# Products over 256 tokens: one 512-column pass for the two halves of the activation

## The chip, the cores and the metric

The program runs on one core of a Trainium2 chip. The metric is the device time of one execution in microseconds (us), over three executions of the same build; less is better.

## The reference

Everything is float32. A sequence of 256 tokens (16 meta tokens go ahead of them, so the first half works on T = 272 rows) of width 2048 passes through four mixers and two feed-forward layers:

- block 1, layer 0: `h = h + mla(rms(h))` (low-rank queries and keys, 16 heads, chunked mask), then `h = h + (silu(g) * u) @ w_down`, with `g, u = split(rms(h) @ w_gu)` and 5632 hidden features;
- block 1, layer 1: `h = h + ((scan(gates(conv(xb))) * gelu(yb)) @ w_o)`, with `xb, yb = split(rms(h) @ w_in)`, then a second feed-forward; from here on only the 256 real tokens are needed;
- a final norm, then block 2, even layer: 8 heads of grouped attention and 8 heads of differential attention (`softmax(s1) - lam * softmax(s2)`) times `silu(gate)`, then `@ w_out_even`;
- block 2, odd layer: 16 heads of windowed attention times `silu(gate)`, `@ w_out_odd`, and a last norm.

Nearly all arithmetic is in products of a weight matrix with the activations of all tokens. The accuracy asked for is near that of float32.

## The kernel before

**The products.** Activations lie with features on the 128 partitions and tokens along the row. Each operand is held as two float32r tensors, a rounded high part and the remainder (low part): `XHt`, `XLt` for the normed input of a stage, `HHt`, `HLt` for the input of its output projection, and `WHt`, `WLt` for the weights. A weight tile of 128x128 times 128 input features of all tokens is three matmuls into one PSUM bank, lines 988 to 990: high weight by high activation, high weight by low activation, low weight by high activation. Each loads its own stationary operand. The moving operand has 272 columns in the first half of the program (`REG`) and 256 later (`REGM`). For the values of the attention heads the operands are swapped (lines 983 to 985, `VT`).

**Units and groups.** Weights come from HBM in 501 units of 1 MB or less, each four 128-row slices by four 128-column tiles as a rule: 16 tile products, 48 matmuls. Each unit is loaded into `raw` by a DMA, split by ACT into `WHt` (line 1194, `split_high`) and by DVE into `WLt` (line 1478, `split_low`). All three have three places. TensorE can start unit n only when DVE has made its `WLt`; ACT can split unit n+3 only when TensorE has finished unit n. A group (`Plan.group`) is four units, or as many as the sum over the input features needs, into four PSUM banks, one per output tile. The eight banks go round in a queue: a group or an attention step takes the bank that was given back longest ago, and TensorE waits (`own`) until that bank's last content has been read.

**The way out.** When a group has ended, its four banks are read by DVE in the feed-forward, the recurrent layer and the gates: `scaled_out` (line 1552) multiplies by the row of inverse norms. `gu_out` does it for the feed-forward, followed by silu on ACT (1304), a product on DVE (1692), the high part on ACT (1308) and the low part on DVE (1694). `qk_out`, `gate_out` and `yg_out` do it for the other products. In output projections `residual` (line 1638) adds the bank to `h`; where a norm follows, ACT makes the next `XHt` (1221) and squares (1237), DVE the next `XLt` (1481), and GpSimd adds the squares (2059). All of that stands ahead of the group's closing `split_high` in ACT's order.

**The order of the work.** `make_plan` writes one list of steps; each engine walks the list and issues its own part of every step, strictly in order. `p.after(k, fn)` puts attention steps k+1 units further on. In the odd layer a head is `s_step` (scores, lines 1122 and 1123, then bias, maximum, exponential and norm), `t_step` (four transposes, line 1130, copied to SBUF by ACT at line 1375) and `v_step` (weighing of values, lines 1139 and 1140). For a pair of heads there are two groups: queries and keys first, then values and gates (`pair_products`).

## Time and profile before

| | |
|---|---|
| median of three executions | 3121.19 us (3121.07 to 3123.58) |
| the profiled execution, its own time | 3122.28 us |
| its span (first to last instruction) | 3120.5 us |
| TensorE matmuls, weight loads | busy 99% and 98% of the span, 25096 records each |
| DVE, ACT, GpSimd | busy 56%, 45%, 4% |
| DMA | 534.89 MB, mean 171 GB/s |
| granted TensorE clock | 0.998 of 2.4 GHz |

The record of a matmul reaches from its first column to its last result, and those of neighbours overlap, so its busy share alone doesn't say how fast TensorE works: the distance from one start to the next does. The chain of waits names what each instruction on it waited for last. "Idle before" is time in which an engine had nothing running, and what ended it.

### The profile page before, as it was taken

Reading aid. Unit: us, or ns where it says so; the run is one execution under the profiler, and the core shown is the slowest. Engines: PE = TensorE matmul, PEld = TensorE weight load, DVE = VectorE, ACT = ScalarE, POOL = GpSimd, SP = SyncE. Lnnn points to the kernel's source line nnn. Section 1 sums busy time; section 2 is a strip of 40 time slices with the busy share of each in tenths; the row PEclk is TensorE's granted clock in tenths of the full one; section 3 lists DMA queues with packets and bytes.
Section 4 is the critical chain, followed back from the end, with each engine's and each line's share of the span. In section 5 each row is a group of like instructions: output and inputs, shape, how many; then the busy total and the mean of one; then the engine's idle time right before and its main releaser. Section 6 shows DMA issues by size and latency. Waiting matters only on the chain.

```text
span 3120.5 us, 56102 instructions
## 1 busy us (share of the span) xinstructions
PE 3088.2 (99%) x25096; PEld 3044.3 (98%) x25096; DVE 1749.4 (56%) x2053; ACT 1394.7 (45%) x1469; POOL 120.1 (4%) x127
## 2 busy tenths in 40 slices
PE   9999999999999999999999999999999999999998
PEld 8889999999999999999999999999999999999998
DVE  6665544444445567755554554555666665555554
ACT  5444433333333456754333333345455554444443
POOL 1001000000000011110000000002000000000000
PEclk9999999999999999999999999999999999999999
DMA  6224454455454554445555555554444445444443
GB/s 227 101 104 149 177 176 175 176 176 176 176 176 174 178 184 185 169 176 191 188 189 189 184 185 186 189 183 178 155 149 149 175 163 189 163 176 163 164 175 122
DMA packets 77888, 534.89 MB, mean 171 GB/s; under 512 B 8528, under 2 KB 11088, under 8 KB 14928
## 3 DMA queue, kind: packets, MB, share of 16 engines
q1 hardware_dynamic: 76640, 528.94, 47.7%
q8 instruction: 197, 3.23, 0.4%
q10 hardware_dynamic: 1008, 2.37, 0.2%
q14 instruction: 43, 0.35, 0.0%
HBM read 529.18 MB, written 2.10 MB: 170 GB/s over the span
## 4 chain that ended last, share of the span: by engine, by line
PE 95%; issue 3%; DVE 1%; ACT 1%; POOL 0%; DMA 0%; SPq 0%; DVEq 0%; ACTq 0%; POOLq 0%
PE PB L988 28%; PE PB L989 28%; PE PB L990 28%; PE PB L983 2%; PE PB L985 2%; PE PB L984 2%; PE PB L1050 0%; PE PB L1090 0%; PE PB L1139 0%; PE PB L1140 0%; PE PB L1051 0%; PE PB L1122 0%; PE PB L1123 0%; DMA raw<-in_mla_in 0%; PE PB L1130 0%
## 5 line engine op out<-in xcount | busy, mean ns | idle before, releaser
L1478 DVE TENSOR_TENSOR WLt<-raw,WHt 128x2048 fp32r<-128x2048 f32 (+2 forms) x506 | 1142.6, 2262 | 938.1 <-ACT WHt L1194 937.7
L1194 ACT ACTIVATE WHt<-raw 128x2048 fp32r<-128x2048 f32 (+2 forms) x506 | 955.4, 1890 | 1298.8 <-PE PB L990 1244.1
L988 PE MATMUL PB<-XHt,WHt 128*128 128x256 f32 (+1 forms) x5072 | 1450.1, 286 | 8.4 <-ACT S L1375 5.8
L989 PE MATMUL PB<-XLt,WHt 128*128 128x256 f32 (+1 forms) x5072 | 1437.5, 283 | 0.0
L990 PE MATMUL PB<-XHt,WLt 128*128 128x256 f32 (+1 forms) x5072 | 1436.0, 283 | 0.0
L988 PEld LDWEIGHTS PB<-XHt,WHt 128*128 128x128 f32 x5072 | 956.0, 188 | 15.3 <-ACT S L1375 8.0
L989 PEld LDWEIGHTS PB<-XLt,WHt 128*128 128x128 f32 x5072 | 955.5, 188 | 2.7 <-issue 1.4
L990 PEld LDWEIGHTS PB<-XHt,WLt 128*128 128x128 f32 x5072 | 954.8, 188 | 0.0
L988 PE MATMUL PB<-HHt,WHt 128*128 128x256 f32 (+1 forms) x2432 | 690.6, 284 | 1.7 <-DVE WLt L1478 0.6
L989 PE MATMUL PB<-HLt,WHt 128*128 128x256 f32 (+1 forms) x2432 | 689.2, 283 | 0.0
L990 PE MATMUL PB<-HHt,WLt 128*128 128x256 f32 (+1 forms) x2432 | 688.5, 283 | 0.0
L988 PEld LDWEIGHTS PB<-HHt,WHt 128*128 128x128 f32 x2432 | 458.0, 188 | 3.0 <-DVE WLt L1478 0.8
L989 PEld LDWEIGHTS PB<-HLt,WHt 128*128 128x128 f32 x2432 | 457.8, 188 | 0.4 <-issue 0.2
L990 PEld LDWEIGHTS PB<-HHt,WLt 128*128 128x128 f32 x2432 | 457.6, 188 | 0.0
L2059 POOL TENSOR_TENSOR acct<-acct,sqt 128x256 f32<-128x256 f32 (+1 forms) x107 | 86.4, 815 | 2785.4 <-ACT sqt L1237 2777.4
L983 PE MATMUL PB<-WHt,XHt 128*128 128x256 f32 (+1 forms) x512 | 147.9, 289 | 0.6 <-DVE S L1570 0.6
L985 PE MATMUL PB<-WLt,XHt 128*128 128x256 f32 (+1 forms) x512 | 143.8, 281 | 0.0
L984 PE MATMUL PB<-WHt,XLt 128*128 128x256 f32 (+1 forms) x512 | 143.5, 280 | 0.0
L1552 DVE TENSOR_TENSOR S<-PB,Rt 128x256 f32<-128x256 f32 (+1 forms) x313 | 114.5, 425 | 26.7 <-PE PB L990 26.5
L983 PEld LDWEIGHTS PB<-WHt,XHt 128*128 128x128 f32 (+1 forms) x512 | 93.9, 183 | 5.1 <-issue 3.4
L1304 ACT ACTIVATE S<-S 128x544 f32<-128x544 f32 (+1 forms) x44 | 28.4, 646 | 157.6 <-DVE S L1552 157.6
L984 PEld LDWEIGHTS PB<-WHt,XLt 128*128 128x128 f32 (+1 forms) x512 | 93.5, 183 | 1.9 <-issue 0.7
(207 smaller groups left out, 1496.7 us busy)
## 6 DMA issues: line engine op xcount, KB each, us to landing
raw<-in_gu SPq DMA_DIRECT2D x176, 1024.0 KB, 4.8
raw<-in_dn SPq DMA_DIRECT2D x88, 1024.0 KB, 4.8
raw<-in_odd_in SPq DMA_DIRECT2D x64, 1024.0 KB, 4.8
raw<-in_even_in SPq DMA_DIRECT2D x52, 1024.0 KB, 4.9
raw<-in_lru_in SPq DMA_DIRECT2D x28, 1024.0 KB, 4.8
raw<-in_mla_o SPq DMA_DIRECT2D x16, 1024.0 KB, 4.9
raw<-in_lru_o SPq DMA_DIRECT2D x16, 1024.0 KB, 4.9
raw<-in_even_o SPq DMA_DIRECT2D x16, 1024.0 KB, 4.8
```

The lines of the kernel that those rows point to most:

```text
L983: t.matmul(o, ah, wh, start=first, stop=False)
L984: t.matmul(o, al, wh, start=False, stop=False)
L985: m = t.matmul(o, ah, wl, start=False, stop=last)
L988: t.matmul(o, wh, ah, start=first, stop=False)
L989: t.matmul(o, wh, al, start=False, stop=False)
L990: m = t.matmul(o, wl, ah, start=False, stop=last)
L1194: a.activation(hi, r, ACT.Copy).then_inc(s_hi, 1)
L1304: a.activation(gg, gg, ACT.Silu).then_inc(sems["silu"], 1)
L1478: v.tensor_tensor(lo, r, hi.bitcast(f32), sub).then_inc(s_lo, 1)
L1552: v.tensor_tensor(dst, PB[b][:, 0:n], by, mult).then_inc(s_bank[b], 1)
L2059: g.tensor_tensor(acc[which][:, t0:T], acc[which][:, t0:T], sq[slot][:, t0:T], add).then_inc(sems["acc"], 1)
```

## The change

A tile kind replaces the flag for swapped operands: "rows" (as before), "values" (swapped) and "wide". For a wide tile the high and the low part of 256 activations are one moving operand of 512 columns, since `Xt` and `Ht` now hold both parts of a feature slice side by side. It meets the high weight in one matmul that fills the whole bank, two halves of 256. The low weight meets the high part in a second matmul, added to the bank's first half. So a tile product is two matmuls instead of three, with the same number of columns. The bank's two halves are added on the way out: ACT copies the second half to SBUF (`halves`), DVE adds the first half to it, and then multiplies two tiles at once by the row of inverse norms (`wide_out`). In output projections DVE adds both halves to `h`, one after the other.

Wide are: all gate and up products of the second feed-forward; three of the four column groups of the four later output projections and of each part of the second feed-forward's; the `y` tiles of the recurrent layer but the last pair; all gates of the attention layers; queries and keys of the odd layer. What works on 272 tokens stays, and so do the fourth column group of each projection, the first attention's queries and the differential attention's queries and keys. In the first attention of the even layer the weighing steps come one unit later, in the odd layer scores and transposes one unit earlier.

```diff
+WIDE = [(128 * c, 128, M0, NT, "wide") for c in range(4)]
...
+    def halves(g, tiles, *where):
+        for i in tiles:
+            p.mark("half", "half", g, i)
+        for i in tiles[1::2]:
+            p.mark("wide", "wide", g, i)
+        p.step("halves", g, tiles, *where)
+
     def out_proj(kunits, t0, fresh, stage, finish=(), scaled=False):
         for m in range(4):
-            g = p.group(kunits, REGM if t0 else REG, "H", 0, fresh if m == 0 else None)
+            g = p.group(kunits, REG if not t0 else WIDE if m < 3 else REGM, "H", 0, fresh if m == 0 else None)
...
-                g = p.group(4, REGM if t0 else REG, "X", 0, stage if j == 0 else None)
+                g = p.group(4, WIDE if t0 else REG, "X", 0, stage if j == 0 else None)
                 for i in range(4):
                     p.give("g", g, i)
+                if t0:
+                    buffers = (2 * (turn % 2), 2 * (turn % 2) + 1)
+                    halves(g, (0, 1, 2, 3), buffers, [last[turn % 2]] if turn > 1 else [])
...
-        tiles = (REG[0:2] if q < 8 else []) + ([REGM[0 if q == 8 else 2], REGM[1 if q == 8 else 3]] if q else [])
+        tiles = (REG[0:2] if q < 8 else []) + (WIDE[2:4] if 0 < q < 8 else REGM[0:2] if q else [])
...
-        g = p.group(4, REGM, "X")
+        g = p.group(4, REGM[0:2] + WIDE[2:4], "X")
...
-        p.after(3, lambda v=v, q=q: (v(0), t_step(("e", 2 * q + 1))))
-        p.after(4, lambda v=v: v(1))
+        p.after(4, lambda v=v, q=q: (v(0), t_step(("e", 2 * q + 1))))
+        p.after(5, lambda v=v: v(1))
...
     def pair_products(name, sides, fresh=None):
-        g = p.group(4, REGM, "X", 0, fresh)
+        odd = name[0] == "C"
+        g = p.group(4, WIDE if odd else REGM, "X", 0, fresh)
         p.close()
...
+        if odd:
+            halves(g, (0, 1, 2, 3), ("q", "k"), done("q_done"))
...
-        g = p.group(4, VT + REGM[:2], "X")
+        g = p.group(4, VT + WIDE[0:2], "X")
...
-        pair_products(("C", q), {2: lambda s=s: s(0), 3: lambda s=s, q=q: (t_step(("o", 2 * q)), s(1)),
+        pair_products(("C", q), {1: lambda s=s: s(0), 2: lambda s=s, q=q: (t_step(("o", 2 * q)), s(1)),
                                  4: lambda v=v, q=q: (v(0), t_step(("o", 2 * q + 1))), 5: lambda v=v: v(1)},
...
-        XHt, XLt = sb("XHt", KD * T, f32r), sb("XLt", KD * T, f32r)
-        HHt, HLt = sb("HHt", KD * T, f32r), sb("HLt", KD * T, f32r)
+        Xt, Ht = sb("Xt", 2 * KD * T, f32r), sb("Ht", 2 * KD * T, f32r)
...
-                        if swap:
+                        if kind == "wide":
+                            o = two(bank[:, :])
+                            both = (X2 if src == "X" else H2)[:, k0 + kk, :, t0:T]
+                            t.matmul(o, wh, both, start=first, stop=False)
+                            m = t.matmul(o[:, 0, :], wl, ah, start=False, stop=last)
+                        elif kind == "values":
...
+            def halves(g, tiles, dst, free):
+                for k in free:
+                    a.wait_ge(*when(*k))
+                for at, i in enumerate(tiles):
+                    b = plan.bank["g", g, i][0]
+                    a.wait_ge(*when("tile", g, i))
+                    a.activation(wide_pairs(dst)[at // 2][:, at % 2, :], PB[b][:, NT:2 * NT], ACT.Copy).then_inc(sems["half"], 1)
...
+            def wide_out(g, tiles, dst, r=None):
+                pairs = wide_pairs(dst)
+                for at, i in enumerate(tiles):
+                    b, x = plan.bank["g", g, i][0], pairs[at // 2][:, at % 2, :]
+                    v.wait_ge(*when("half", g, i))
+                    v.tensor_tensor(x, PB[b][:, 0:NT], x, add).then_inc(s_bank[b], 1)
+                if r:
+                    v.wait_ge(*when(*r))
+                for x, i in zip(pairs, tiles[1::2]):
+                    v.wait_ge(*when("out", "g", g, i - 1))
+                    v.wait_ge(*when("out", "g", g, i))
+                    v.tensor_tensor(x, x, RO.unsqueeze(1).to_broadcast([128, 2, NT]), mult).then_inc(sems["wide"], 1)
...
+                if plan.groups[g][2][i][4] == "wide":
+                    then(v.tensor_tensor(h[:, mt, t0:T], PB[b][:, NT:2 * NT], h[:, mt, t0:T], add))
+                    v.wait_ge(s_vec, vec[0])
                 v.tensor_tensor(h[:, mt, t0:T], PB[b][:, 0:T - t0], h[:, mt, t0:T], add).then_inc(s_bank[b], 1)
```

TensorE at the end of a pair of the odd layer (`Xt` is the new tensor of both parts). Before, transposes of the first head and scores of the second stand between the values-and-gates group and the next pair's first group:

```order
L988 MATMUL PB<-XHt,WHt 128x256
L989 MATMUL PB<-XLt,WHt 128x256
L990 MATMUL PB<-XHt,WLt 128x256
L1130 MATMUL PB<-cst,S 128x128 x4
L1122 MATMUL PB<-S 128x256
L1123 MATMUL PB<-S 128x256
```

Now the same steps stand inside the values-and-gates group, with its last unit (swapped products, then wide ones) behind them:

```order
L1004 MATMUL PB<-Xt,WHt 128x512
L1005 MATMUL PB<-Xt,WLt 128x256
L1155 MATMUL PB<-cst,S 128x128 x4
L1147 MATMUL PB<-S 128x256
L1148 MATMUL PB<-S 128x256
L1008 MATMUL PB<-WHt,Xt 128x256
L1009 MATMUL PB<-WHt,Xt 128x256
L1010 MATMUL PB<-WLt,Xt 128x256
```

The gate product of three matmuls has become two, one of 512 columns, and one unit of products now lies between these steps and the next group. Over the whole program TensorE's list goes from 24521 to 20761 rows.

ACT at the end of the second feed-forward, before (silu, high part, the four weight splits of the next four units):

```order
L1304 ACTIVATE S<-S 128x512
L1308 ACTIVATE HHt<-S 128x2x256
L1194 ACTIVATE WHt<-raw 128x2048 x4
L1304 ACTIVATE S<-S 128x512
L1308 ACTIVATE HHt<-S 128x2x256
```

and now:

```order
L1281 ACTIVATE S<-PB 128x256 x4
L1337 ACTIVATE S<-S 128x512
L1341 ACTIVATE Ht<-S 128x2x256
L1219 ACTIVATE WHt<-raw 128x2048 x4
L1281 ACTIVATE S<-PB 128x256 x4
```

Four copies of half a bank (L1281) stand ahead of each silu, and so ahead of the split of the weights that comes after the high part.

## Rows read from the trace of the kernel before

**Rows 1.** The page: busy time, then the chain that ended last

```profile
PE 3088.2 (99%) x25096; PEld 3044.3 (98%) x25096; DVE 1749.4 (56%) x2053; ACT 1394.7 (45%) x1469; POOL 120.1 (4%) x127
...
PE 95%; issue 3%; DVE 1%; ACT 1%; POOL 0%; DMA 0%; SPq 0%; DVEq 0%; ACTq 0%; POOLq 0%
```

**Rows 2.** Windows: second feed-forward (256 columns), first (272); start:end, length, busy (count)

```profile
core 0: us, PE busy (x) PEld busy (x) DVE busy (x) ACT busy (x) POOL busy (x), PEclk, DMA share, GB/s
1430.00:1590.00 160.00, 160.00 (x1362) 160.00 (x1361) 86.53 (x72) 63.78 (x44) 0.00 (x0) 1.00 0.54 189
...
350.00:500.00 150.00, 150.00 (x1198) 150.00 (x1198) 77.13 (x66) 55.36 (x40) 0.00 (x0) 1.00 0.49 174
```

**Rows 3.** Chain in order of time: plain float32 products, start and length

```profile
1305.46 1.83 PE PB L1090 x8
...
2205.72 0.86 PE PB L1103 x2
```

**Rows 4.** Groups of instructions, shapes apart: count, busy us, mean ns

```profile
L989 PE MATMUL PB<-XLt,WHt 128*128 128x256 f32 x3104 | 869.2, 280 | 0.0
...
L989 PE MATMUL PB<-XLt,WHt 128*128 128x272 f32 x1968 | 568.3, 289 | 0.0
```

**Rows 5.** Timeline of TensorE: stationary operand of 16 columns, then of 128

```profile
151.51 0.28 PE L983 MATMUL PB<-WHt,XHt 128*16 128x256 f32 x1
151.63 0.28 PE L984 MATMUL PB<-WHt,XLt 128*16 128x256 f32 x1
151.74 0.28 PE L985 MATMUL PB<-WLt,XHt 128*16 128x256 f32 x1
151.86 0.28 PE L983 MATMUL PB<-WHt,XHt 128*128 128x256 f32 x1
```

**Rows 6.** TensorE's waits for ACT: total us, times, longest

```profile
PE PB L988 <- ACT S L1375: 6.3, 12, 0.5
```

**Rows 7.** Timeline: start of a pair of the odd layer

```profile
2661.62 0.28 PE L990 MATMUL PB<-XHt,WLt 128*128 128x256 f32 x1
2661.82 0.58 ACT L1375 ACTIVATE S<-PB 128x512 f32<-128x512 f32 x1
...
2662.44 0.39 PE L988 MATMUL PB<-XHt,WHt 128*128 128x256 f32 x1 [0.54 <-ACT S L1375]
```

**Rows 8.** Groups of instructions, shapes apart: reading and scaling of banks

```profile
L1552 DVE TENSOR_TENSOR S<-PB,Rt 128x256 f32<-128x256 f32 x184 | 66.5, 419 | 10.0 <-PE PB L990 9.9
...
L1638 DVE TENSOR_TENSOR ht<-PB,ht 128x256 f32<-128x256 f32 x96 | 36.0, 425 | 16.8 <-PE PB L990 16.8
...
L1692 DVE TENSOR_TENSOR S<-S 128x512 f32<-128x512 f32 x22 | 15.2, 693 | 2.3
...
L1356 ACT ACTIVATE S<-PB,sml 128x256 f32<-128x256 f32 x26 | 10.7, 460 | 0.0
```

**Rows 9.** Timeline of DVE and ACT: end of a group, second feed-forward

```profile
1463.95 1.43 DVE L1552 TENSOR_TENSOR S<-PB,Rt 128x256 f32<-128x256 f32 x4 [0.34 <-PE PB L990]
...
1468.68 2.29 DVE L1478 TENSOR_TENSOR WLt<-raw,WHt 128x2048 fp32r<-128x2048 f32 x1 [1.11 <-ACT WHt L1194]
...
1466.75 1.90 ACT L1194 ACTIVATE WHt<-raw 128x2048 fp32r<-128x2048 f32 x1
```

**Rows 10.** Timeline of DVE and ACT: end of a column group, second feed-forward's last projection

```profile
2130.18 1.50 DVE L1638 TENSOR_TENSOR ht<-PB,ht 128x256 f32<-128x256 f32 x4 [0.27 <-PE PB L990]
...
2139.65 4.49 DVE L1478 TENSOR_TENSOR WLt<-raw,WHt 128x2048 fp32r<-128x2048 f32 x2 [5.89 <-ACT WHt L1194]
...
2130.64 1.71 ACT L1221 ACTIVATE XHt<-ht,sml 128x256 fp32r<-128x256 f32 x4 [3.06 <-DVE ht L1638]
...
2137.72 3.71 ACT L1194 ACTIVATE WHt<-raw 128x2048 fp32r<-128x2048 f32 x2
```

**Rows 11.** Timeline of DVE: the first column group there, then the even layer's projection

```profile
2113.24 1.50 DVE L1638 TENSOR_TENSOR ht<-PB,ht 128x256 f32<-128x256 f32 x4 [0.27 <-PE PB L990]
...
2121.81 4.49 DVE L1478 TENSOR_TENSOR WLt<-raw,WHt 128x2048 fp32r<-128x2048 f32 x2 [5.49 <-ACT WHt L1194]
...
2566.80 1.50 DVE L1638 TENSOR_TENSOR ht<-PB,ht 128x256 f32<-128x256 f32 x4
...
2573.33 4.50 DVE L1478 TENSOR_TENSOR WLt<-raw,WHt 128x2048 fp32r<-128x2048 f32 x2 [2.95 <-ACT WHt L1194]
```

More of the change, by code:

```diff
@@ L632, in make_plan @@
         p.mark("silu", "silu", "A", q)
-        p.step("gate_silu", gb, ("A", q), ("out", "g", g, 3))
+        p.step("gate_silu", gb, ("A", q), ("wide", g, 3))
         q_in = ("out", "g", g, 1)
@@ L729, in pair_products @@
         p.mark("silu", "silu", name)
-        p.step("gate_silu", "gp", (name,), ("out", "g", g, 3))
+        p.step("gate_silu", "gp", (name,), ("wide", g, 3))
         cur["silu"] = ("silu", name)
@@ L814, in flat @@
             return x.rearrange("p a n -> p (a n)")
-        h, XH, XL, HH, HL = three(ht), three(XHt), three(XLt), three(HHt), three(HLt)
+        h = three(ht)
+        X2, H2 = (t[:, :].rearrange("p (k s n) -> p k s n", k=KD, s=2) for t in (Xt, Ht))
+        XH, XL, HH, HL = X2[:, :, 0, :], X2[:, :, 1, :], H2[:, :, 0, :], H2[:, :, 1, :]
         ident, ones, perm = cst[:, 0:128], cst[:, 128:256], cst[:, 256:384]
@@ L869, in build_program, with wide_pairs @@
         RO = R[:, M0:T]
+        def wide_pairs(dst):
+            return [yg] if dst == "yg" else [two(buf[x] if x in buf else gbuf[x][:, 0:2 * NT]) for x in dst]
         def last_sq(mt):
@@ L966, in unit @@
                 for k, ti in order:
-                    for c0, wd, t0, tn, swap in (tiles[ti],):
+                    for c0, wd, t0, tn, kind in (tiles[ti],):
                         kk = ku * nk + k
@@ L1302, in gu_out @@
                 gg, u = two(gbuf[2 * turn][:, 0:2 * n]), two(gbuf[2 * turn + 1][:, 0:2 * n])
-                a.wait_ge(*when("out", "g", g, 1))
+                a.wait_ge(*when(*(("wide", g, 1) if t0 else ("out", "g", g, 1))))
                 a.activation(gg, gg, ACT.Silu).then_inc(sems["silu"], 1)
@@ L1423, in _ @@
                     c_split(*x)
+                elif what == "halves":
+                    halves(*x)
                 elif what == "uq_out":
@@ L1687, in gu_out @@
                     v.wait_ge(*when(*r))
-                for i in range(4):
-                    scaled_out((gg, u)[i // 2][:, i % 2, :], g, i, None, n, R[:, t0:T])
+                if t0:
+                    wide_out(g, (0, 1, 2, 3), (2 * turn, 2 * turn + 1))
+                else:
+                    for i in range(4):
+                        scaled_out((gg, u)[i // 2][:, i % 2, :], g, i, None)
                 v.wait_ge(*when("silu", l, j))
-                v.wait_ge(*when("out", "g", g, 3))
+                v.wait_ge(*when(*(("wide", g, 3) if t0 else ("out", "g", g, 3))))
                 v.tensor_tensor(u, u, gg, mult).then_inc(sems["gu"], 1)
@@ L1828, in kA_scale, with gate_out, qk_out @@
                 v.tensor_tensor(buf["kA"], buf["kA"], PB[b][:, :], mult).then_inc(s_bank[b], 1)
-            def gate_out(b, g, free):
+            def gate_out(b, g):
+                wide_out(g, (2, 3), (b,))
+            def qk_out(g, free, r):
                 for k in free:
                     v.wait_ge(*when(*k))
-                for i in range(2):
-                    scaled_out(two(buf[b])[:, i, :], g, 2 + i, None, NT, RO)
-            def qk_out(g, free):
-                for k in free:
-                    v.wait_ge(*when(*k))
-                for i in range(4):
-                    r = ("out", "sp", "ln_odd") if i == 0 else None
-                    scaled_out(two(buf[("q", "k")[i // 2]])[:, i % 2, :], g, i, r if odd[0] else None, NT, RO)
-            odd = [False]
+                if plan.groups[g][2][0][4] == "wide":
+                    wide_out(g, (0, 1, 2, 3), ("q", "k"), r)
+                else:
+                    for i in range(4):
+                        scaled_out(two(buf[("q", "k")[i // 2]])[:, i % 2, :], g, i, None, NT, RO)
             def rows(q, before):
```

32 lines of the change are left out of this document (18 added, 14 removed).

## The prediction

> **What bounds the kernel.** I read the page first. TensorE is busy for 99% of the span, and 95% of the chain of waits is its matmuls; DVE is at 56% and ACT at 45% [rows 1]. The time is therefore a number of matmuls times their pace, plus the few places where TensorE stands. The pace I took from windows without attention. In the second feed-forward 1362 matmuls overlap 160 us; two of them were already running, so the distance from start to start is 160/1360 = 117.6 ns for 256 columns. In the first it is 150/1196 = 125.4 ns for 272 [rows 2]. At the granted 2.4 GHz, one column per cycle, 256 columns take 106.7 ns and 272 take 113.3. So 10.9 and 12.1 ns of each matmul are not columns. The change keeps every column and removes matmuls, so it can gain only from this remainder, and all depends on what the remainder is.
>
> **Part 1, fewer and longer matmuls.** The wide tile products are 22 groups x 64 in the second feed-forward, 92 feature slices x 12 tiles in the projections, 224 in the recurrent layer, 256 in the even layer's gates, 768 in the odd layer: 1408 + 1104 + 224 + 256 + 768 = 3760, which is what TensorE's list loses (24521 to 20761). Each was 3 x 117.6 = 352.9 ns.
>
> No row shows a 512-column matmul of this type. The two paces bound it. If the remainder belongs to the matmul, the long one takes 213.3 + 10.9 = 224.2 ns and a product saves 10.9. If the pace grows per column as it does from 256 to 272 columns, by 7.8/16 = 0.49 ns, it takes 117.6 + 256 x 0.49 = 242.4 ns, against 235.3 for two: a loss of 7.1 ns. The ends are +41 us and -27 us over 3760.
>
> The nearest rows of 512 columns are plain float32 products, at two cycles per column: eight records of 272 columns in 1.83 us are 228.8 each, 2.1 over their cycles; two of 512 in 0.86 us are 430 each, 3.3 over their 426.7 [rows 3]. There, what is over hardly grows with length: it is per matmul. It isn't the weight load either, since with a stationary operand of 16 columns the distance is still (151.86 - 151.51)/3 = 0.117 us [rows 5]. I take the side of a cost per matmul, but not all of it: going by 272 against 256 columns, 1.2 ns more for 16 more, some grows. I count 9.2 ns saved per product, an estimate between these rows: 3760 x 9.2 = **34.6 us**.
>
> **Part 2, the moved steps.** TensorE waits 12 times for ACT's copy of transposed weights (L1375) [rows 6]: once per pair of the odd layer, 8, and 4 in the first attention. The transposes stood directly ahead of a group, and the group's third tile is given the bank that they had just filled. At one such place the start of the tile comes at 2662.44, 0.82 us after its predecessor at 2661.62 instead of 0.12 [rows 7], so 0.70 us is lost. Now a unit of products (5.6 us) follows the transposes, and the copy is long done when the bank comes round: 12 x 0.70 = **8.4 us** gained.
>
> The scores of the odd layer come one unit earlier, two units (11 us) behind the query group. Queries and keys are ready later than before: split of weights on ACT to 1.9 us, four copies of 0.46, the last add at 4.2, two multiplications of 0.69 to 5.6 us [rows 8]. 5 us remain. The softmax chain, scores to transposes, keeps its one unit. I count nothing.
>
> **Part 3, the longer way out.** ACT gets 166 copies of half a bank (88 in the feed-forward, 14 recurrent, 16 even, 48 odd), at the 0.46 us of a similar read, 76 us. DVE gets 83 multiplications of 512 elements at 0.69 (the 166 old multiplications become adds), 57 us, and 72 second adds in projections at 0.425, 31 us [rows 8]. The cover is TensorE: ACT goes to 48%, DVE to 60% of the time. What counts is how late `WLt` of the unit three ahead becomes. In the feed-forward the group ends near 1464.75, and the units in hand last 2 x 5.65 = 11.3 us, until 1476.05. The split of the high part starts at 1466.75 and DVE's low part ends at 1470.97 [rows 9]: 5.1 us of margin. Copies from -1.0 to +0.85 us, last add at 1.3, first product 2.0, silu 2.6, product 3.4, high part 4.05, split 5.95, low part 8.25, that is 2 us later than now: margin about 2.8 with the shorter units. Free; if this cover went, each of 22 groups would cost what is missing.
>
> One place is tight: the last projection of the second feed-forward, where ACT squares everything twice ahead of its split. The group ends near 2131.05, the units in hand last until 2142.35; the first of DVE's two low parts ends at 2139.65 + 2.29 = 2141.94 [rows 10]. Margin 0.4 us, and ACT is the one that is late (its split starts at 2137.72). Now each `XHt` waits for two adds; eight adds of 0.375 take until 2133.1, the fourth `XHt` ends at 2133.6 instead of 2132.35, 1.2 us later, and the two units are 0.3 us shorter. Missing: 1.1 us, at two of three column groups. At the first the adds begin at 2113.24, the units in hand last until 2125.4 and the low part ends at 2121.81 + 2.25 = 2124.1, a margin of 1.3, and 0.2 is missing. **2.5 us** lost. The other projections square once: their low part ends 8.8 us after the adds begin (2566.80 to 2575.6), a margin of 3.4, and nothing is missing [rows 11].
>
> **Sum.** Against the profiled execution's own 3122.28 us (span 3120.5): 3122.3 - 34.6 - 8.4 + 2.5 = 3081.8. That run lies 1.1 us above the median 3121.19, so **3081 us**.
>
> **Rivals.**
>
> *A. The remainder goes with the columns.* For it: a matmul's own record is 280 ns at 256 columns and 289 at 272 [rows 4]; less the paces, 162 and 164: the extra time lies within the record, not between records, as if the columns came more slowly than one per cycle. Then only the part that plain float32 products show, 2.1 to 3.3 ns, is saved: 3760 x 2.3 = 8.6 us, 3121.2 - 8.6 - 8.4 + 2.5 = **3107 us**. Against it: record ends are modelled, and at 272 columns the remainder should be 11.6, not 12.1. The Trainium skill (TensorE: Matmul & The Clock Gate, Back-to-back issue gap) gives columns/2.4 + 2.5 ns per matmul, which speaks against this change: it would save 2.5 x 3760 = 9.4 us, to 3106. The trace disagrees with its pace, 117.6 ns instead of 109.2. Chance 0.23.
>
> *B. The long matmul costs more than two short ones* (the other side). The growth of 0.49 ns per column holds on to 512: 242.4 ns. For it: it is the only slope that rows give for this type, and the moving operand is now two pieces that lie apart. Then 3121.2 + 26.7 - 8.4 + 2.5 = **3142 us**. It decides for slower by over 0.2% above 238.5 ns for the long matmul. Against: 0.49 is more than a cycle per column, which leaves a negative cost per matmul. Chance 0.15.
>
> *C. The merge gives nothing*: the chip treats the two-piece operand as two passes, and the change doesn't do what it says. The gain is the moved steps, 3121.2 - 5.9 = **3115 us**; a few short waits for DVE or ACT at group ends, of 0.1 us each at some 60 groups, would make that 3121. Chance 0.10.
>
> *D. More gain.* The remainder comes from a weight load that just fails to fit under 256 columns, and fits under 512: the long matmul takes 213.3 + 3.3, 18.7 ns saved, 70 us, **3045 us**. Rows 5 speak against it. Chance 0.06.
>
> **How the numbers follow.** My forecast (a cost per matmul) has 0.46. About 0.2%, 6 us, is what a measurement of this kernel can tell from no change: faster are my case, A and D, 0.75; within it is C, 0.10; slower B, 0.15. My own case runs from 3070 (12.1 ns saved) to 3091 (6.5 ns). The range takes in A and C and the nearer edge of B: 3060 to 3130, leaving out D and most of B.
>
> **What would show it.** In the window of the second feed-forward a tile product (two matmuls) every 341 to 344 ns is my case, 350 is A, 353 C, 360 B, 334 D. The record of the 512-column matmul should be about 387 ns (224 + 163), against 396 under A. The 12 waits for L1375 should be gone. In the last projection of the second feed-forward TensorE should wait about 1 us for `WLt` at two or three places, and nowhere in the other groups. The prediction is wrong if the product's pace lies above 350 ns, or if waits of TensorE for `WLt`, banks or queries add up to more than 5 us.

## The result, and the profile after

| | before | after |
|---|---|---|
| median of six executions each | 3122.07 us (3121.07 to 3123.58) | 3110.59 us (3108.75 to 3111.82) |
| ratio, 95% interval | | 0.9962 (0.9951 to 0.9973) |
| the profiled execution, span | 3122.28, 3120.5 us | 3111.64, 3109.8 us |

The changed kernel is faster by 11.5 us, inside the range, but the forecast was 41 us. The page of the changed kernel, busy time and the chain of waits (for before, rows 1):

```profile
PE 3080.9 (99%) x21336; PEld 2871.8 (92%) x21336; DVE 1828.5 (59%) x2208; ACT 1448.7 (47%) x1635; POOL 110.7 (4%) x127
...
PE 95%; issue 2%; DVE 1%; ACT 1%; POOL 1%; ACTq 0%; DVEq 0%; POOLq 0%
```

TensorE has 3760 records less and is still busy for 99% of the time: its busy time fell by only 7.3 us. DVE and ACT took on nearly what Part 3 said (59% and 47%). So the question is the pace. The same two windows as in [rows 2]:

```profile
core 0: us, PE busy (x) PEld busy (x) DVE busy (x) ACT busy (x) POOL busy (x), PEclk, DMA share, GB/s
350.00:500.00 150.00, 150.00 (x1197) 150.00 (x1196) 76.21 (x65) 56.09 (x39) 0.00 (x0) 1.00 0.49 174
1430.00:1590.00 160.00, 160.00 (x914) 139.45 (x913) 95.54 (x86) 73.55 (x73) 0.00 (x0) 1.00 0.52 189
```

In the second feed-forward 914 matmuls overlap 160 us, two of them were already running: 912/2 = 456 products, 350.9 ns each. Before it was 3 x 117.6 = 352.9. By the starts in the trace a unit of 16 wide products takes 5.613 us, 350.8 ns per product, against 5.6465 us, 352.9 ns. **A merged product saves 2.1 ns**, where 9.2 were counted. One row behind the other, the changed kernel's timeline of TensorE:

```profile
1499.95 0.39 PE L1004 MATMUL PB<-Xt,WHt 128*128 128x512 f32 x1
1500.18 0.28 PE L1005 MATMUL PB<-Xt,WLt 128*128 128x256 f32 x1
1500.30 0.40 PE L1004 MATMUL PB<-Xt,WHt 128*128 128x512 f32 x1
1500.54 0.28 PE L1005 MATMUL PB<-Xt,WLt 128*128 128x256 f32 x1
```

From a wide pass to the next matmul are 0.23 to 0.24 us, 232.5 ns on average from 1432 to 1660 us, from a narrow one 0.12 (118.3 ns). The narrow pass is nearly what it was; the wide pass costs 232.5, nearly the 235.2 of the two passes that it replaces. The waits of TensorE in the changed kernel (total us, times, longest), where [rows 6] stood:

```profile
PE PB L1004 <- DVE WLt L1513: 2.3, 3, 1.3
...
PE PB L1115 <- DVE S L1773: 1.7, 1, 1.7
...
PE PB L1013 <- DVE WLt L1513: 1.2, 1, 1.2
```

No wait for a copy of transposes is left; before there were 12, 6.3 us. New are waits for `WLt` (0.6 us before, 3.5 now) and 1.1 us more for `S` at the head of the recurrent layer's last gates (L1115; L1090 with 0.6 us before). Three of the four `WLt` waits stand behind the three merged column groups of the second feed-forward's last projection, the places of [rows 10, 11]:

```profile
2124.16 0.50 PE L1004 MATMUL PB<-Ht,WHt 128*128 128x512 f32 x1 [0.30 <-DVE WLt L1513]
...
2142.56 0.51 PE L1004 MATMUL PB<-Ht,WHt 128*128 128x512 f32 x1 [1.32 <-DVE WLt L1513]
...
2161.00 0.39 PE L1013 MATMUL PB<-Ht,WHt 128*128 128x256 f32 x1 [1.24 <-DVE WLt L1513]
```

The fourth, 0.67 us at the start of the recurrent layer's projection, was there before with 0.64.

The starts of the stages in the two traces say where the span's 10.7 us came from: up to the recurrent layer +1.9, recurrent layer with its projection +0.2, second feed-forward -0.3, even layer's products and attention -3.4, its projection -0.4, odd layer's products and attention -7.3, the rest -1.4. The two stages in which steps were moved hold -3.4 and -7.3, as much as the whole. In the second feed-forward, where half of all merges are, two things cancel: up to its last projection it is 3.7 us shorter (1792 merged products x 2.1 ns are 3.8), and the last projection, with its three waits, is 3.4 us longer. And the first 1124 us, where nothing is merged, became longer.

### The profile page after: what moved, and what is told of

The parts are those of the page before. It is cut to its first block, busy times and chain, and to the rows that moved or that the text cites. A ratio compares the mean times of both kernels' runs of the same rounds, so it can differ in the third digit from the quotient of the medians.

```text
span 3109.8 us, 49013 instructions
## 1 busy us (share of the span) xinstructions
PE 3080.9 (99%) x21336; PEld 2871.8 (92%) x21336; DVE 1828.5 (59%) x2208; ACT 1448.7 (47%) x1635; POOL 110.7 (4%) x127
## 4 chain that ended last, share of the span: by engine, by line
PE 95%; issue 2%; DVE 1%; ACT 1%; POOL 1%; ACTq 0%; DVEq 0%; POOLq 0%
PE PB L1004 27%; PE PB L1013 15%; PE PB L1015 15%; PE PB L1014 14%; PE PB L1005 13%; PE PB L1008 2%; PE PB L1010 2%; PE PB L1009 2%; PE PB L1147 0%; PE PB L1075 0%; PE PB L1164 0%; PE PB L1155 0%; PE PB L1165 0%; PE PB L1148 0%; POOL acct L2112 0%
## 5 line engine op out<-in xcount | busy, mean ns | idle before, releaser
L1004 PE MATMUL PB<-Xt,WHt 128*128 128x512 f32 x2656 | 949.9, 395 | 0.0
L1005 PE MATMUL PB<-Xt,WLt 128*128 128x256 f32 x2656 | 744.3, 280 | 0.0
L1013 PE MATMUL PB<-Xt,WHt 128*128 128x272 f32 (+1 forms) x2416 | 704.5, 292 | 2.5 <-DVE Xt L1516 1.9
L1015 PE MATMUL PB<-Xt,WLt 128*128 128x272 f32 (+1 forms) x2416 | 694.6, 287 | 0.0
L1014 PE MATMUL PB<-Xt,WHt 128*128 128x272 f32 (+1 forms) x2416 | 693.2, 287 | 0.0
L1004 PEld LDWEIGHTS PB<-Xt,WHt 128*128 128x128 f32 x2656 | 498.6, 188 | 101.2
L1005 PEld LDWEIGHTS PB<-Xt,WLt 128*128 128x128 f32 x2656 | 499.1, 188 | 0.2
L1013 PEld LDWEIGHTS PB<-Xt,WHt 128*128 128x128 f32 x2416 | 455.8, 189 | 13.2 <-DVE WLt L1513 3.0
L1014 PEld LDWEIGHTS PB<-Xt,WHt 128*128 128x128 f32 x2416 | 457.1, 189 | 2.3 <-issue 1.4
L1015 PEld LDWEIGHTS PB<-Xt,WLt 128*128 128x128 f32 x2416 | 456.7, 189 | 0.0
L1004 PE MATMUL PB<-Ht,WHt 128*128 128x512 f32 x1104 | 389.7, 396 | 2.6 <-DVE WLt L1513 2.3
L1013 PE MATMUL PB<-Ht,WHt 128*128 128x272 f32 (+1 forms) x1328 | 380.4, 286 | 1.2 <-DVE WLt L1513 1.2
L1014 PE MATMUL PB<-Ht,WHt 128*128 128x272 f32 (+1 forms) x1328 | 379.3, 286 | 0.0
L1004 PEld LDWEIGHTS PB<-Ht,WHt 128*128 128x128 f32 x1104 | 207.2, 188 | 53.8 <-DVE WLt L1513 3.7
L1013 PEld LDWEIGHTS PB<-Ht,WHt 128*128 128x128 f32 x1328 | 249.7, 188 | 1.8 <-DVE WLt L1513 1.4
L1014 PEld LDWEIGHTS PB<-Ht,WHt 128*128 128x128 f32 x1328 | 250.2, 188 | 0.0
L1015 PEld LDWEIGHTS PB<-Ht,WLt 128*128 128x128 f32 x1328 | 250.0, 188 | 0.0
L1005 PEld LDWEIGHTS PB<-Ht,WLt 128*128 128x128 f32 x1104 | 207.2, 188 | 0.3 <-issue 0.2
```

What stands on the lines that cost most here:

```text
L1004: t.matmul(o, wh, both, start=first, stop=False)
L1005: m = t.matmul(o[:, 0, :], wl, ah, start=False, stop=last)
L1013: t.matmul(o, wh, ah, start=first, stop=False)
L1014: t.matmul(o, wh, al, start=False, stop=False)
L1015: m = t.matmul(o, wl, ah, start=False, stop=last)
```

## The experiments

Medians are of repeated executions beside the kernel before on the same chip; the three programs of matmuls alone ran once each. Where runs of different sets are compared, their kernels before differ by up to 0.5 us (3122.07 to 3122.55).

### The pace of one matmul

A program of matmuls alone, 192 of each form, without waits:

```diff
+ for i in range(192): t.matmul(o[:, 0:256], W[:, w:w + 128], X4[:, k, i % 2, 16:272])
+ for i in range(192): t.matmul(o[:, 0:272], W[:, w:w + 128], X4[:, k, i % 2, 0:272])
+ for i in range(192): t.matmul(o[:, 0:n], W[:, w:w + 128], X[:, 512 * k:512 * k + n])
+ for i in range(192): t.matmul(o (two halves), W[:, w:w + 128], X4[:, k, :, 16:272])
```

> A kernel of matmuls alone, float32r, 160 to 192 in a row of each form, a new weight tile for each unless said; it computes nothing of the reference. Forms: 256, 272, 320, 384 and 512 columns; 512 as two pieces of 256; 256 with always the same weights; 256 with a stationary operand of 32 columns; 256 with every matmul opening its own sum; bfloat16 at 256 and 512 columns; 256 and 512 again beside a busy ScalarE and VectorE. Theory 1 (the part beyond one column per cycle goes with the columns at four bytes each, about 2 ns are per matmul): 512 columns 231 to 234 ns from start to start, 320 about 146, 384 about 175, bfloat16 109 at 256 and 216 at 512, and neither pieces, weights, the short stationary operand nor busy neighbours change 256 columns by over 2 ns. Theory 2 (a cost of 9 to 11 ns per matmul): 512 columns 224, 320 144, 384 171, bfloat16 near 117 at 256. Theory 3 (0.49 ns per column beyond 256): 512 columns 242, 384 180.

`X4` has rows of two parts of 272, so its row k starts at element 544k; `X` is read here in rows that start at 512k, with n = 320, 384 and 512. Its timeline of TensorE: start, length, line, form, count. Start to start, divided by 192, is the pace.

```profile
43.88 22.72 PE L844 MATMUL PB<-X,W 128*128 128x256 f32 x192
66.44 24.32 PE L846 MATMUL PB<-X,W 128*128 128x272 f32 x192
90.60 28.32 PE L848 MATMUL PB<-X,W 128*128 128x320 f32 x192
118.75 33.47 PE L850 MATMUL PB<-X,W 128*128 128x384 f32 x192
152.06 43.72 PE L852 MATMUL PB<-X,W 128*128 128x512 f32 x192
195.62 44.70 PE L854 MATMUL PB<-X,W 128*128 128x512 f32 x192
240.16 22.72 PE L856 MATMUL PB<-X,W 128*128 128x256 f32 x192
262.71 22.72 PE L858 MATMUL PB<-X,W 128*32 128x256 f32 x192
...
307.84 21.13 PE L862 MATMUL PB<-Xb,Wb 128*128 128x256 bf16 x192
328.81 41.60 PE L864 MATMUL PB<-Xb,Wb 128*128 128x512 bf16 x192
```

| form (float32r) | pace, ns | over one column per cycle |
|---|---|---|
| 256, 16 elements into rows of 272 | 117.5 | 10.8 |
| 272, from the start of such rows | 125.8 | 12.5 |
| 320, 384, 512 in one piece at 512k | 146.6, 173.5, 226.9 | 13.3, 13.5, 13.5 |
| 512 in two pieces, 272 apart, from 544k + 16 (L854) | 232.0 | 18.7 |

With operands at 512k the remainder is a fixed amount per matmul from 320 to 512 columns, as I had held; it does not go with the columns there (rival A gave 232 to 233 for 512, and 226.9 came out). But it is larger than the short pass's in its old place, and for the operand of the changed kernel larger again, by 5.1 ns. Two old passes take 235.0 ns, the new one 232.0: 3.0 ns are saved where 9.2 were counted (2.1 in the program). In the kernel's own rows, at 544k, no width between 272 and 512 was measured, so whether the remainder grows with the columns in that place is open. The same weights every time (L856) or only 32 columns of weights (L858) change nothing, which ends rival D.

In bfloat16 256 columns take 109.2 ns and 512 take 215.8 (first start at 328.81, last at 370.04, 191 steps), 2.5 over their cycles at both lengths. There the trace agrees with the formula in the Trainium skill (TensorE: Matmul & The Clock Gate, Back-to-back issue gap), columns/2.4 + 2.5 ns; for the float32r of this kernel it does not. The same section of the Trainium skill calls that formula the gap of an isolated matmul and gives about 131 ns at 512 columns for a stream of weight loads and matmuls; this stream of 192, a new weight tile each, shows 215.8 instead.

### The moved steps alone

The kernel before, with the steps moved:

```diff
-        p.after(3, lambda v=v, q=q: (v(0), t_step(("e", 2 * q + 1))))
-        p.after(4, lambda v=v: v(1))
+        p.after(4, lambda v=v, q=q: (v(0), t_step(("e", 2 * q + 1))))
+        p.after(5, lambda v=v: v(1))
...
-        pair_products(("C", q), {2: lambda s=s: s(0), 3: lambda s=s, q=q: (t_step(("o", 2 * q)), s(1)),
+        pair_products(("C", q), {1: lambda s=s: s(0), 2: lambda s=s, q=q: (t_step(("o", 2 * q)), s(1)),
```

> The kernel before with the attention steps moved and nothing else. If nearly all of the gain came from the moved steps: 10 to 11 us less than before (ratio about 0.9966), all of it in the first attention and the odd layer, and no wait of TensorE for L1375. If the merged products gave most of it: 3 us less or nothing.

3112.94 us against 3122.45, ratio 0.9968 (0.9956 to 0.9981): -9.5 us, 6 to 14 by that interval. The waits for L1375 are gone; the first of TensorE's waits in its trace is now

```profile
PE PB L1000 <- POOL acct L2059: 2.4, 2, 1.2
```

which was there before. Part 2's 8.4 us fits, and most of what the change brings is here.

### The merges without the moves

The changed kernel with those lines put back:

```diff
-        p.after(4, lambda v=v, q=q: (v(0), t_step(("e", 2 * q + 1))))
-        p.after(5, lambda v=v: v(1))
+        p.after(3, lambda v=v, q=q: (v(0), t_step(("e", 2 * q + 1))))
+        p.after(4, lambda v=v: v(1))
...
-        pair_products(("C", q), {1: lambda s=s: s(0), 2: lambda s=s, q=q: (t_step(("o", 2 * q)), s(1)),
+        pair_products(("C", q), {2: lambda s=s: s(0), 3: lambda s=s, q=q: (t_step(("o", 2 * q)), s(1)),
```

> The changed kernel with the attention steps where they were before. Theory 1 (a merged product saves 2.1 ns, 7.9 us in all, and the new waits and the new layout take back most of it): within 3 us of before, with the 12 waits of 0.7 us back or somewhat longer ones. A cost per matmul: 25 to 35 us less than before.

3119.28 us, ratio 0.9988 (0.9980 to 0.9997): -3.2 us. Its waits and its pace:

```profile
PE PB L1004 <- ACT S L1408: 5.9, 11, 0.6
...
PE PB L1004 <- DVE WLt L1513: 2.3, 3, 1.3
```

```profile
1430.00:1590.00 160.00, 160.00 (x914) 139.48 (x913) 95.54 (x86) 73.21 (x73) 0.00 (x0) 1.00 0.52 190
```

The twelfth wait, 0.5 us, now stands on another line. The two parts add within the measurement: -9.5 - 3.2 = -12.7, against -11.5 for both.

### The layout alone

The kernel before, with high and low part side by side and nothing merged:

```diff
-        XHt, XLt = sb("XHt", KD * T, f32r), sb("XLt", KD * T, f32r)
-        HHt, HLt = sb("HHt", KD * T, f32r), sb("HLt", KD * T, f32r)
+        Xt, Ht = sb("Xt", 2 * KD * T, f32r), sb("Ht", 2 * KD * T, f32r)
```

> The kernel before with high and low parts side by side in one tensor, and nothing else. If the layout alone slows the three-matmul products: units of 256 columns 5.653 us instead of 5.647 and of 272 columns 6.025 to 6.031 instead of 6.020, together 2 to 4 us more than before (501 units, 5 to 10 ns each). If those differences are the clock of the run: the same as before within 1 us, and the units too.

3126.31 us, ratio 1.0011 (1.0002 to 1.0020): **+3.9 us** (0.6 to 6.2 by that interval; every execution lies above every one of before) for moving the operands to other addresses. Its waits are those of before; a unit of 48 matmuls takes, by the starts in the trace, 5.653 us instead of 5.6465 at 256 columns and up to 6.031 instead of 6.020 at 272. The changed kernel's first 1124 us, +1.9 us, have the same layout and nothing else new.

### The new waits taken away

Three passes kept in the second feed-forward's last projection and at the recurrent layer's last pair:

```diff
-            g = p.group(kunits, REG if not t0 else WIDE if m < 3 else REGM, "H", 0, fresh if m == 0 else None)
+            g = p.group(kunits, REG if not t0 else WIDE if m < 3 and stage != "ln_even" else REGM, "H", 0, fresh if m == 0 else None)
...
-        tiles = (REG[0:2] if q < 8 else []) + (WIDE[2:4] if 0 < q < 8 else REGM[0:2] if q else [])
+        tiles = (REG[0:2] if q < 8 else []) + (WIDE[2:4] if 0 < q < 7 else REGM[2:4] if q == 7 else REGM[0:2] if q else [])
```

> The changed kernel with three matmuls per product again in two places: the projection ahead of the even layer (whose group ends are followed by twice the squares) and the last pair of y tiles in the recurrent layer. If the long way out costs a wait there: units of 7.1 us in that projection go back to 5.65, 2.9 us, and 1.1 us in the recurrent layer, less 0.4 us for 176 products that cost 2.1 ns more: about 3107. If those waits were hidden anyway: 3111.

3106.95 us, ratio 0.9949 (0.9937 to 0.9962), 3.6 us below the changed kernel. Its wait for `WLt` on that line:

```profile
PE PB L1004 <- DVE WLt L1513: 0.7, 1, 0.7
```

That wait was there before, with 0.6 us. So the cost that Part 3 named is real and of its size, and in these two places together, which were not tried apart, the merges cost more than they give.

### One piece instead of two

The first pace program seemed to ask for a contiguous operand; this run and the next program were planned together, before either had a result. In the changed kernel, from the recurrent layer's projection on:

```diff
+        X3, H3 = (t[:, 0:2 * KD * NT].rearrange("p (k s n) -> p k s n", k=KD, s=2) for t in (Xt, Ht))
```

High and low part now touch, and every row of 512 starts at a multiple of 512 elements.

> The changed kernel with the high and low part of the 256 tokens directly beside each other (512 columns in one piece) from the recurrent layer's output projection on; the recurrent layer's own products stay in two pieces. If the two pieces cost 5 to 6.6 ns per merged product: 3536 products x 6.6 = 23 us less than the change, about 3088. If they cost nothing in the kernel: 3111 as the change.

3118.89 us, ratio 0.9987 (0.9978 to 0.9996): **8 us slower than the changed kernel**, where 3088 had been expected. With the waits taken away too, by the edit of the section above:

> Both edits. If they are independent: 23 and 3 us less than the change, about 3085, below both kernels. If the shorter products turn the margins at group ends into waits: 3090 or more, with waits of TensorE for WLt beyond those of the change.

3117.14 us, ratio 0.9982 (0.9973 to 0.9991), a miss by as much. The waits for `WLt` go away as before (0.9 us left), and both runs show the same two windows, so the cause is likely one. The windows of the dense kernel's second feed-forward:

```profile
1430.00:1590.00 160.00, 160.00 (x925) 139.91 (x924) 95.58 (x87) 75.17 (x74) 0.00 (x0) 1.00 0.52 192
1700.00:1860.00 160.00, 160.00 (x908) 138.82 (x907) 91.94 (x84) 71.93 (x71) 0.00 (x0) 1.00 0.51 185
```

The same code runs at 346.7 ns per product in one stretch (923/2 products) and at 353.2 in another (906/2); by starts its units take 5.547 or 5.650 us, and those of plain passes 5.760 instead of 5.653. That is not a wait and not the clock (granted 1.00 in both). By the starts, in this stage the merged products average 350.7 ns, as in the changed kernel (350.8). The loss is elsewhere: some 760 plain products behind the recurrent layer take 6.3 ns more, 4.8 us, and merged ones in the attention stages 356.0 instead of 349.2 (even layer) and 352.7 instead of 349.9 (odd layer).

### What the place of the operand does

Two more programs of matmuls alone. In the first, among others:

```diff
+ t.matmul(o[:, 0:256], W[:, w:w + 128], X[:, 512 * k:512 * k + 256])            L844
+ t.matmul(o[:, 0:256], W[:, w:w + 128], X[:, 512 * k + 16:512 * k + 272])       L846
+ t.matmul(o[:, 0:256], W[:, w:w + 128], X[:, 544 * k:544 * k + 256])            L848
+ t.matmul(o[:, 0:512], W[:, w:w + 128], X[:, 512 * k + 16:512 * k + 528])       L852
+ t.matmul(o[:, 0:512], W[:, w:w + 128], X[:, 544 * k:544 * k + 512])            L854
+ t.matmul(o[:, 0:512], W[:, w:w + 128], X[:, 544 * k + 16:544 * k + 528])       L856
+ t.matmul(o (two halves), W[:, w:w + 128], X4[:, k, :, 0:256])                  L858
+ t.matmul(o (two halves), W[:, w:w + 128], (256 at 256 * k, 256 at 256 * k + 2048))  L860
+ t.matmul(o[:, 0:512], W[:, w:w + 128], X[:, 512 * k:512 * k + 512])            L862
+ t.matmul(o[:, 0:256], W[:, 1920 - w:2048 - w], X[:, 512 * k:512 * k + 256])    L863
```

> Matmuls alone again, float32r, a new weight tile each, only the place and the pieces of the moving operand changed; it computes nothing of the reference. The first such kernel gave 117.5 ns at 256 columns in rows of 272, 226.7 at 512 in one piece starting at a multiple of 512, 231.9 at 512 in two pieces 272 apart. Theory P (each further piece costs about 5 ns): 512 in one piece stays at 226.7 wherever it starts, two pieces are 232 wherever they lie, also at multiples of 256 and far apart. Theory Q (the start against 2 KB or 1 KB boundaries costs it): 512 in one piece but 16 columns off is 230 or more, two pieces at multiples of 256 are 227, and 256 columns at a multiple of 512 differ from 117.5. Pairs of a 512-column and a 256-column matmul, as in the changed kernel: 344 ns dense, 350 in pieces.

The timeline of its TensorE:

```profile
44.57 23.20 PE L844 MATMUL PB<-X,W 128*128 128x256 f32 x192
67.61 22.78 PE L846 MATMUL PB<-X,W 128*128 128x256 f32 x192
90.23 22.74 PE L848 MATMUL PB<-X,W 128*128 128x256 f32 x192
112.81 24.23 PE L850 MATMUL PB<-X,W 128*128 128x272 f32 x192
136.87 44.12 PE L852 MATMUL PB<-X,W 128*128 128x512 f32 x192
180.83 44.64 PE L854 MATMUL PB<-X,W 128*128 128x512 f32 x192
225.31 44.56 PE L856 MATMUL PB<-X,W 128*128 128x512 f32 x192
269.70 44.74 PE L858 MATMUL PB<-X,W 128*128 128x512 f32 x192
314.28 43.70 PE L860 MATMUL PB<-X,W 128*128 128x512 f32 x192
357.82 0.39 PE L862 MATMUL PB<-X,W 128*128 128x512 f32 x1
...
391.73 0.40 PE L866 MATMUL PB<-X,W 128*128 128x512 f32 x1
```

256 columns at 512k (L844) take (67.61 - 44.57)/192 = 120.0 ns each, 16 elements further on (L846) 117.8. The same division gives for 512 columns:

| moving operand | 512 columns, ns | twice 256 columns in that place | a merge saves, ns |
|---|---|---|---|
| one piece at 512k | 226.9 (first program) | 240.0 | 13.1 |
| one piece at 512k + 16 (L852) | 229.0 | 235.6 | 6.6 |
| one piece at 544k (L854) | 231.7 | 235.2 | 3.5 |
| one piece at 544k + 16 (L856) | 231.2 | 235.0 | 3.8 |
| two pieces 272 apart, at 544k (L858) | 232.2 | 235.2 | 3.0 |
| two pieces 2048 apart, at 256k (L860) | 226.8 | | |

So it is not the pieces (Theory P) but the place (Theory Q): one piece in the changed kernel's rows is as slow as two to within 1 ns, and two pieces in a good place are as fast as one. The 5.1 ns of the first program belong to the row start at 544k, and the 23 us expected of the dense kernel rested on a cost of the pieces that is not there. What a merge saves depends on the place as well.

And 96 pairs of a dense 512-column pass and a 256-column one, both at 512k, take (391.73 - 357.82)/96 = 353.2 ns, though each alone takes 226.9 and 120.0, 346.9 in all. The pair is not the sum of its parts; 344 had been expected, and 350 for the pair in pieces, which takes 351.1. The second tries other offsets s:

```diff
+ t.matmul(o[:, 0:512], W[:, w:w + 128], X[:, 512 * k + s:512 * k + s + 512])
+ t.matmul(o[:, 0:256], W[:, 1920 - w:2048 - w], X[:, 512 * k + s:512 * k + s + 256])
```

> A kernel of matmuls alone, like the two pace kernels; it computes none of the reference. After a warm-up, 96 matmuls each of 256 float32r columns at 512k plus 1, 4, 8, 24 and 32 elements (k the row of the operand), then pairs as the changed kernel has them, a pass of 512 columns and one of 256 on the same data, 96 of each: one piece at 512k plus 4, plus 8 and plus 16; one piece at 512k whose narrow pass takes the second half; one piece at 512k whose narrow pass starts 16 elements on; two pieces 272 apart from the row's start; two pieces 512 apart from 256k; four wide passes followed by four narrow ones, at 512k; last, two pieces 272 apart from 16 elements on, as the changed kernel has them. Theory P, the place of the operand sets the fixed part of a pass: what starts at a multiple of 512 elements takes its columns plus 32 at 2.4 GHz (120.0 and 226.7 ns, as the two pace kernels measured), what starts between takes 117.5 at 256 and 229 to 232 at 512, by the offset within 32 elements. It expects 120.0 at plus 32, 117 to 118 at plus 1 to 24; pairs of 346 to 347 with one piece at 512k, whichever half the narrow pass takes, and 344 to 345 if it starts 16 elements on; pairs of 349 to 351 for one piece at plus 4 to 16 and for two pieces. Rival Q, the fixed part belongs to the change of width: all pairs take 350 to 353 wherever they start, and four wide and four narrow passes in a row take 4 x 346.7, less than the pairs do.

Its timeline: the starts of the blocks of 96 (L844 to L852 single 256-column passes, L854 on pairs).

```profile
43.99 11.99 PE L844 MATMUL PB<-X,W 128*128 128x256 f32 x96
55.81 11.37 PE L846 MATMUL PB<-X,W 128*128 128x256 f32 x96
...
67.02 11.37 PE L848 MATMUL PB<-X,W 128*128 128x256 f32 x96
...
78.22 11.68 PE L850 MATMUL PB<-X,W 128*128 128x256 f32 x96
89.73 11.56 PE L852 MATMUL PB<-X,W 128*128 128x256 f32 x96
101.13 0.39 PE L854 MATMUL PB<-X,W 128*128 128x512 f32 x1
...
134.42 0.39 PE L857 MATMUL PB<-X,W 128*128 128x512 f32 x1
...
167.71 0.39 PE L860 MATMUL PB<-X,W 128*128 128x512 f32 x1
...
201.60 0.39 PE L863 MATMUL PB<-X,W 128*128 128x512 f32 x1
...
335.61 0.86 PE L875 MATMUL PB<-X,W 128*128 128x512 f32 x3
...
369.29 0.39 PE L881 MATMUL PB<-X,W 128*128 128x512 f32 x1
```

| operand starts at 512k plus | 256 alone, ns | pair 512 + 256, ns |
|---|---|---|
| 0 (the run before this) | 120.0 | 353.2 |
| 1 | 123.1 | |
| 4 | 116.8 | 346.8 |
| 8 | 116.7 | 346.8 |
| 16 | 117.8 (the run before) | 353.0 |
| 24 | 119.9 | |
| 32 | 118.8 | |

The place decides, but not by the rule that I had written down: plus 24, plus 32 and plus 1 came out otherwise, pairs at plus 16 are slow and not fast, and the pair of one piece whose narrow pass takes the second half is at 353.3. The rival falls too: four wide and four narrow passes in a row (L875) take 4 x 350.8, more than the best pairs. Two pieces 512 apart from 256k, and one piece at 512k whose narrow pass starts 16 elements on, take 346.7 per pair, as the best do; two pieces 272 apart from the row's start take 349.2. What remains is a table of measured places: in the pair, 8 elements of shift save 6 ns against the dense kernel and 4 against the two pieces of the changed kernel (350.6).

### The same 8 elements in the kernel

```diff
-        X3, H3 = (t[:, 0:2 * KD * NT].rearrange(...) for t in (Xt, Ht))
+        X3, H3 = (t[:, 8:8 + 2 * KD * NT].rearrange(...) for t in (Xt, Ht))
```

> The dense kernel (high and low part of an operand row next to each other, rows 512 elements apart, from the recurrent stage's last projection on) with the whole operand moved by 8 elements; nothing else differs. The last pace kernel ran the pair of a 512- and a 256-column pass in 346.8 ns with one piece at 512k + 8, in 353.1 or 346.7 at 512k, in 350.6 with the two pieces of the changed kernel; 256 columns took 116.7 ns at 512k + 8, 120.0 at 512k. Theory P, the place decides: some 3540 merged products (those of the recurrent pairs keep the old place) x 4 ns and some 35 units' worth of 256-column products x 0.05 us less than the changed kernel's 3110.6: 3094 us, ratio 0.991; the unit of merged products is 5.547 us everywhere, never 5.650, and the unit of plain ones 5.60. Rival Q, the pairs alone show this and in the program the weight copies and evictions beside them undo it: units of both 5.55 and 5.65, and a time between the changed and the dense kernel, 3110 to 3119.

3095.66 us, ratio 0.9916 (0.9902 to 0.9929): 23.2 us less than the dense kernel by one offset, 14.9 less than the changed kernel. Theory P's 3094 holds to 2 us. The windows of its second feed-forward, at the places where the dense kernel had 925 and 908:

```profile
1430.00:1590.00 160.00, 160.00 (x925) 141.83 (x924) 95.91 (x86) 74.63 (x72) 0.00 (x0) 1.00 0.53 193
1700.00:1860.00 160.00, 160.00 (x925) 141.86 (x924) 93.00 (x86) 73.12 (x71) 0.00 (x0) 1.00 0.52 189
```

346.7 ns in both; units of 5.547 us, and of 5.600 for plain passes. With the three-pass edits of the run without the new waits on top:

> The same, with three passes per product kept in the last projection before the even layer and at the last pair of the recurrent stage, as in the kernel without the stalls, which took 3106.95 us. Theory P: 3.3 us below the shifted kernel, 3091 us, ratio 0.990. Rival R, a faster product leaves the weight preparation and the evictions less time, so that the waits that were removed come back at other places: 3094 or more, with over 3 us of waits for WLt, Xt or S that the changed kernel doesn't have.

3091.01 us (3090.96 to 3091.76), ratio 0.9902 (0.9888 to 0.9915). **This version beats both kernels**, by 31 and by 20 us. The waits that were taken away do not come back elsewhere: for `WLt` 1.0 us are left on the line of the wide pass,

```profile
PE PB L1009 <- DVE WLt L1518: 1.0, 2, 0.8
```

Last, what the merge itself is worth there. The wide pass is split, and nothing else:

```diff
-                            t.matmul(o, wh, both, start=first, stop=False)
+                            t.matmul(o[:, 0, :], wh, both[:, 0, :], start=first, stop=False)
+                            t.matmul(o[:, 1, :], wh, both[:, 1, :], start=False, stop=False)
```

> The shifted kernel without the stalls, with one line changed: the 512-column pass of a merged product is issued as two passes of 256 columns, into the same two halves of the bank, so that evictions, halves added on the way out, waits and placement stay and the merge alone goes. It separates what the merge gives from what the placement gives. Theory P: a product takes 3 x 116.7 = 350.1 ns instead of 346.8, so 3600 x 3.4 ns = 12 us more than the shifted kernel without the stalls: 3103 us, ratio 0.994; the unit is 5.60. Rival G, my sum's: a merge saves the 9 ns that a 256-column pass costs above its columns: 32 us more, 3123 us. Rival N, placement does it all and the merge gives nothing: 3091 us, as without the edit.

3103.95 us (3103.22 to 3105.29), ratio 0.9944 (0.9930 to 0.9957): 12.9 us more. Theory P's 3103 came true. The window:

```profile
1430.00:1590.00 160.00, 160.00 (x1374) 160.00 (x1373) 95.54 (x86) 73.67 (x72) 0.00 (x0) 1.00 0.53 191
```

1372/3 products, 349.9 ns each against 346.7. In this place the merge is worth 3.2 ns per product, 12.9/3600 = 3.6 by the times. Rival G, the 9 ns of my sum, would have been 32 us; rival N, nothing. This kernel without any merged pass is 9.0 us below the moved steps alone (3112.94): that is what the place gives, less what the longer way out costs. The kernel before with the shifted rows and nothing else was not tried.

## Why the prediction was wrong

**Part 1, -34.6 us, failed.** The step is "I count 9.2 ns saved per product". Measured are 2.1 ns, 3760 x 2.1 = 7.9 us. Wrong was to carry the remainder of the *short* pass over to the long one. It is not one number: 10.8 ns for 256 columns in the old place, 13.5 for 512 at 512k, 18.7 for 512 in the changed kernel's place, where one piece takes 17.9 (231.2 ns) too. The mechanism, a cost per matmul that is neither the weight load nor per column, is shown for operands at 512k: 13.3 ns at 256 columns, 12.0 at 272 (L850 of the second program) and 13.3 to 13.5 at 320, 384 and 512. In the kernel's own rows only 256, 272 and 512 were measured, and there it is not shown. The operand's place stood in no term of the sum. I had read the step from 256 to 272 columns as a little growth with length; but [rows 2] compare two places as well as two lengths. The float32 products of [rows 3] said that it is fixed, and nothing about its size here.

**Part 2, -8.4 us, was right**: -9.5 us alone, all 12 waits gone, nothing late in their place.

**Part 3 was right in kind and place.** The cover holds in all 22 groups of the second feed-forward. The last projection waits 0.3 us where 0.2 was missing and 1.3 and 1.2 where 1.1 was, 2.9 us in all. The prediction's own three terms make 2.4, not the 2.5 that it wrote. Not seen was the recurrent layer's last pair, +1.1 us. Taking both away gave 3.6 us, with the savings of 176 merges gone as well.

**Missing from the sum** was the new layout as such: I costed it at nothing without naming it. Alone it costs 3.9 us; about 1.5 of that (the 3760 merged products are 235 units' worth, x 0.0065 us) falls on products that are merged in the changed kernel and whose pace is counted above, which leaves 2.4.

The sum by what the runs show: -7.9 - 9.5 + 3.6 + 2.4 = -11.4 us, where 11.5 were measured. That they meet to 0.1 us is in part luck: the intervals of the single runs reach 3 to 4 us to each side. The stages of the two traces agree with it: twelve waits of 0.7 us are 2.8 in the even layer's attention and 5.6 in the odd one's, and 2.1 ns for each of their 256 and 768 merges makes that 3.3 and 7.2, where 3.4 and 7.3 are seen.

**The rivals.** A's figures nearly came true, 350 ns per product (350.9), a record of 396 ns (395 to 396), 3107 us (3110.6); its reason is not shown. At 512k it is wrong, since 512 columns take 226.9 ns there; in the kernel's place the long pass costs what A says (232.0 against 232 to 233), and whether by columns or by the place, no run tells. One piece or two is not the reason. B (242 ns) is excluded by 232, C (nothing gained) by the 2.1 ns and, in the shifted place, by the three-pass run, D by the forms with other weights. I had written that a product's pace above 350 ns would mean a wrong prediction; it is 350.9.

## What to carry to other kernels

Before merging passes, measure the merged pass with its own operand, pieces, stride and offset included: a fixed cost that is read off the short pass is not that of the long one, and in the rows of one width alone a merge saved anything from 3.0 to 13.1 ns by the place of its operand. When a layout changes, price it by itself, with nothing else changed; here the dense rows moved by 8 elements were worth 14.9 us against the changed kernel, and all merges in that place 12.9. A wait that is one step late in the order of the work, repeated 12 times, was the cheapest gain in this change, and the trace of before had its size.

## What the runs showed of the hardware

- The pace of a float32r matmul depends on where its moving operand starts: 256 columns took from 116.7 to 123.1 ns at the offsets tried, 512 in one piece 226.9 at 512k, 229.0 sixteen elements further on (43.96 us for 192) and 231.7 at 544k. Whether the 512 columns lie in one piece or two made at most 1 ns. Why these offsets and not others is open; I have a table and no rule.
- The same dense code settles at one of two paces, 346.7 or 353.2 ns per product, and keeps it for dozens of units. In both dense runs the second feed-forward is at the fast one up to 1660 us and at the slow one from 1700 on (60 us windows: 348 and 342 matmuls), with a column group of plain passes between; in no window within a run of merged products did it change. At plus 8 both windows show the fast one. What chooses between them was not tried.
- bfloat16 shows a remainder of 2.5 ns at both lengths; that its pace would not depend on the place was not tried.
- Busy DVE and ACT beside TensorE changed nothing: 117.5 and 226.7 ns from start to start in the last blocks of the first pace program, with both engines busy over 98% of the time, as without them.
